# Where the weight slots and the feed-forward tiles begin in SBUF, modulo 512 bytes

## The reference, cut to what matters

```python
for i in range(DEPTH):            # first block
    h = rms_norm(x, attn_norm_g[i])
    q, k, v, u, vv = split(h @ w_in[i])
    merged = concat(rms_norm(gqa_attention(q, k, v)), rms_norm(spatial_gating(u, vv)))
    x = x + merged @ w_o[i]
    h = depthwise_conv(rms_norm(x, ffn_norm_g[i]) @ w_up[i])     # 2 x 2816 columns, 3 taps
    x = x + (silu(gate) * up) @ w_down[i]
for i in range(DEPTH):            # second block
    z = rms_norm(x) @ w_in_2[i]
    mix = concat(dilated_attention, conformer_conv, gated_deltanet)(z)
    x = x + rms_norm(mix @ w_out_2[i])
    h = rms_norm(x)
    x = x + rms_norm((silu(h @ w_gate_2[i]) * (h @ w_up_2[i])) @ w_down_2[i])
```

## Time and profile before

| | |
|---|---|
| median of 3 runs | 2637.12 us (2636.78 to 2638.16) |
| the profiled execution | 2636.79 us |
| its span, first to last instruction | 2635.0 us |
| TensorE busy | 2551.0 us, 97% |
| VectorE, ScalarE, GpSimd busy | 57%, 42%, 5% |
| mean granted TensorE clock | 0.989 of full speed |
| read from HBM | 205.34 MB, 79 GB/s over the span |

### The profile page before, as it was taken

The page is one execution under the profiler, slowest core; times in us unless marked ns, Lnnn a source line. Parts: engine busy times, 40 slices in busy tenths (PEclk is TensorE's granted clock), DMA queues, the critical chain, the costliest instruction groups (busy, mean ns, idle before and its releaser), DMA issues.

```text
span 2635.0 us, 36784 instructions
## 1 busy us (share of the span) xinstructions
PE 2551.0 (97%) x12956; PEld 2021.1 (77%) x12966; DVE 1514.5 (57%) x1957; ACT 1105.3 (42%) x1602; POOL 134.1 (5%) x119
## 2 busy tenths in 40 slices
PE   7999999999999999999998899999899999899998
PEld 5767888887668888887678778888676787688886
DVE  4656755756556746656975554344559755543444
ACT  4554433435554424432475443232424754431323
POOL 1000000000000000000212010000102120100000
PEclk9999999999999999999999999999999999999998
DMA  4203332333113333342220223333221201233333
GB/s 133 72 1 89 98 108 87 99 93 93 49 33 92 102 93 96 100 115 64 56 65 11 64 77 104 91 96 106 55 77 52 65 18 56 72 101 90 96 99 92
DMA packets 394592, 208.04 MB, mean 79 GB/s; under 512 B 9738, under 2 KB 392660, under 8 KB 394484
## 3 DMA queue, kind: packets, MB, share of 16 engines
q1 hardware_dynamic: 391396, 202.79, 26.7%
q0 software_dynamic: 2176, 3.06, 0.5%
q10 hardware_dynamic: 912, 0.77, 0.1%
HBM read 205.34 MB, written 2.10 MB: 79 GB/s over the span
## 4 chain that ended last, share of the span: by engine, by line
PE 89%; DVE 6%; ACT 3%; issue 1%; DMA 0%; SPq 0%; DVEq 0%; ACTq 0%
PE ps L622 65%; PE ps L641 6%; PE ps L899 2%; DVE ps L2773 1%; DVE x_sb L2776 1%; ACT whi L1449 1%; PE ps L1052 1%; PE ps L1067 1%; DVE yc L2497 1%; DVE h_lo L2767 1%; PE ps L1227 1%; PE ps L954 1%; PE ps L1205 1%; PE ps L956 1%; PE ps L955 1%
## 5 line engine op out<-in xcount | busy, mean ns | idle before, releaser
L1449 ACT ACTIVATE whi<-raw 128x1024 fp32r<-128x1024 f32 (+1 forms) x354 | 395.8, 1119 | 1071.2 <-PE ps L622 947.5
L622 PE MATMUL ps<-h_hi,whi 128*128 128x512 f32 x1984 | 789.2, 398 | 4.7 <-ACT whi L1449 4.1
L622 PE MATMUL ps<-h_lo,whi 128*128 128x512 f32 x1984 | 773.7, 390 | 0.0
L622 PE MATMUL ps<-h_hi,wlo 128*128 128x512 f32 x1984 | 530.3, 389 | 0.0
L2095 DVE TENSOR_TENSOR wlo<-raw,whi 128x1024 fp32r<-128x1024 f32 (+1 forms) x354 | 458.7, 1296 | 56.2 <-ACT whi L1449 55.1
L622 PEld LDWEIGHTS ps<-h_hi,whi 128*128 128x128 f32 x1984 | 373.3, 188 | 89.7 <-ACT whi L1449 8.2
L622 PEld LDWEIGHTS ps<-h_lo,whi 128*128 128x128 f32 x1984 | 373.2, 188 | 82.7 <-issue 6.2
L622 PEld LDWEIGHTS ps<-h_hi,wlo 128*128 128x128 f32 x1984 | 372.5, 188 | 77.2
L622 PE MATMUL ps<-a_hi,whi 128*128 128x512 f32 x592 | 230.3, 389 | 0.0
L622 PE MATMUL ps<-a_lo,whi 128*128 128x512 f32 x592 | 230.3, 389 | 0.0
L2808 DVE TENSOR_TENSOR cv<-ps,rstd 128x512 f32<-128x512 f32 x88 | 60.9, 692 | 248.9 <-PE ps L622 241.0
(11 more groups left out here) (408 smaller groups left out, 3281.0 us busy)
## 6 DMA issues: line engine op xcount, KB each, us to landing
raw<-in_w_up SPq DMA_DIRECT2D x132, 512.0 KB, 3.8
raw<-in_w_down SPq DMA_DIRECT2D x64, 704.0 KB, 4.5
raw<-in_w_in SPq DMA_DIRECT2D x82, 512.0 KB, 3.8
raw<-in_w_gate SPq DMA_DIRECT2D x44, 512.0 KB, 3.8
raw<-in_w_o SPq DMA_DIRECT2D x16, 512.0 KB, 3.7
raw<-in_w_out SPq DMA_DIRECT2D x16, 512.0 KB, 3.7
xs<-in_x SPq DMA_DIRECT2D x2, 1024.0 KB, 6.8
out<-xs SPq DMA_DIRECT2D x3, 512.0 KB, 2.9
```

The costliest lines, as they stand in the source:

```text
L622: return pe.matmul(ps[:, ACC[s], :], w[s][:, k, :], r[:, k, :], start=start, stop=stop)
L1449: act.activation(whi[s][:, 0:kt, :], raw[s][:, 0:kt, :], ACT.Copy).then_inc(w_hi_ready.sem, 1)
```

## The change

Dummy tensors are put between others; nothing reads or writes them. The order of `whi` and `wlo` changes from whi0, whi1, wlo0, wlo1 to whi0, wlo0, whi1, wlo1. No instruction is added, removed or moved.

```diff
-        whi = [sb(f"whi{s}", [P, HALF, P], F32R) for s in range(2)]
-        wlo = [sb(f"wlo{s}", [P, HALF, P], F32R) for s in range(2)]
+        whi, wlo = [], []
+        for s in range(2):
+            sb(f"phase{s}", [P, 112])
+            whi.append(sb(f"whi{s}", [P, HALF, P], F32R))
+            wlo.append(sb(f"wlo{s}", [P, HALF, P], F32R))
+        sb("phase_rest", [P, 32])
...
         with ExitStack() as on:
+            sb("phase_a", [P, 32], on=on)
             a_hi = sb("a_hi", [P, HALF, SEQ], F32R, on=on)
             a_lo = sb("a_lo", [P, HALF, SEQ], F32R, on=on)
```

## The result

The changed kernel takes 2668.7 us (median, 2667.62 to 2672.36) against 2637.37 us: 1.0121 times, 95% interval 1.0104 to 1.0139. It is slower by 31 us, 1.2%. The forecast was no change, 2637 us, with its own range of 2632 to 2642; the time lies outside that and inside the whole range of 2610 to 2680, which was wide enough to hold the slower rival.

What follows compares the result with a forecast made beforehand. TensorE, busy 97%, was taken to bound the kernel through 9024 dense matmuls at 226.67 ns. Casts 0 and pitch change 0 x 9024 summed to 0, so 2637 us; own range 2632 to 2642, whole range 2610 to 2680.

Steps and rivals of the forecast that it cites:

- the slower rival: Every `unit`, lines 622 and 641: out-of-phase data stops the stream settling at 226.67 ns; 2674 or 2676 us; chance 0.27.
- The bound: Whole kernel: TensorE busy 97%; 9024 dense matmuls at 226.67 ns pitch are on the path, 9.02 us per ns.
- Weight casts and low parts: ScalarE and VectorE producing `whi` (1060 ns) and `wlo` (1224 ns): out-of-phase source and target cost 0.
- The matmul stream: Dense float32r matmuls: pitch stays 226.67 ns despite new data-to-weight distances; 0 x 9024 = 0, bounds -105 to +120 us.
- I take 0: Dense matmul pitch: no change, since all tiles share one pitch and line 999's short load costs no less.
- the row that I called nearest: The chain's piece of 726 dense matmuls, `h` and `a` tiles, even and odd units: 164.56 us, 226.67 ns each.
- The bounds, 215 and 240 ns: Dense matmul pitch: lowest from the float32 pair, -105 us; highest from the unsettled stretch's longest step, +120 us.
- The rule on ports: TensorE's SBUF reads: moving operand and LDWEIGHTS have independent ports, so by the cited skill page the sum is 0.
- The loss of the settled state: The slower rival: dense stream no longer settles, pitch +4.1 or +4.3 ns, +37 or +39 us; chance 0.27, other slowdowns included.
- The argument against it: Against lost settling: the unsettled stretch after a float32 matmul had the settled one's phases, so phase alone doesn't make the state.
- The faster rival: Dense matmuls: the 13.3 ns are the two reads meeting in phase and go; 2532 us if all reach 215 ns; chance 0.20.

Runs made afterwards that it cites:

- 64-column runs: `unit` loads 64 weight columns instead of 128, half of each output tile left out: 2659.61 us with the addresses of the kernel before, 2662.47 us with the changed kernel's.

## Why the prediction was wrong

**The bound.** Right: the loss is in the pitch of the dense matmuls and lands on the end nearly whole. 3.9 ns of mean pitch x 9024 = 35 us, of 31 measured; the scale of 9.02 us for each nanosecond held within what waiting and unsettled stretches took off.

**Weight casts and low parts.** Right: 1060 and 1224 ns before and after.

**The matmul stream.** Here the forecast failed, in the step "I take 0", on both of its reasons. The first was that h and a tiles, hi and lo, both slots all had one pitch at many addresses. All of them had distance 0, so they were one sample and not six; the row that I called nearest held nothing on the question. What the runs showed in place of 0 is +2.1, +6.5, +6.7 and +0.4 ns at the distances 64, 128, 192 and 256, the mean of the dense pitch going from 227.0 to 230.9 ns. The second was that the short load of line 999 costs no less than the long one, so that the two reads would not meet. The 64-column runs show the inference void: there too the shorter load costs more in phase (230.0 against 226.67), and its pitch still depends on the distance. The bounds, 215 and 240 ns, held; the measured classes lie between 227 and 233. The upper one was a reading of starts rounded to 10 ns: the longest step of that unsettled stretch is 236 ns, the shortest 224.

**The rule on ports.** The rule from the Trainium skill, page "SBUF — State Buffer", section "Who interferes with whom", that TensorE's two read ports are independent and only the VectorE and GpSimd pair contends, does not cover this kernel. Nothing but the distance between the two operands' addresses was changed, by one side or by the other, and the pitch moved by up to 7.4 ns; moved together, it did not. The measurement decides.

**The rivals.** The loss of the settled state was what happened, priced at 230.8 to 231.1 ns, +37 to +39 us; measured were 230.9 ns and +31 us. The whole was mis-sized by what before already paid in unsettled stretches, 3 us, and by the 2.7 us of waiting that went. That the mean pitch met the price is luck: it is the mean of 228.8, 233.1, 233.3 and 227.0, and no class ran at the price. The argument against it, that the unsettled stretch of before had the same phases as the settled one, was true and beside the point: with a good phase the stream settles within nine steps, with another it does not within a unit. I gave this rival 0.27. Line 999, a product at mixed distances that did not settle, was the one row with another distance; it deserved to be the row that I leaned on.
The faster rival failed: of the eight residues none is under 226.67 at 512 columns. The 216 ns that the Trainium skill's page "TensorE: Matmul & The Clock Gate", section "Back-to-back issue gap", gives for a single warm matmul of 512 columns were reached at no phase.

**What stays open.** That the streamed data and the weight load meet in SBUF, every 256 bytes, is the reading that fits: the effect needs both addresses, repeats, changes with the load's length, and is gone at half clock (426 or 427 ns at distances 288 and 352, as at 0). No run shows the meeting itself, and why the cycles have the lengths that they have is not explained. Nor were distances finer than 32 bytes tried.

## What to carry to other kernels

Before calling addresses harmless, ask at how many distances the trace has the two operands: rows that agree because all share one alignment are one sample. Where float32r matmuls run back to back on 512 columns with 128-column loads, keep data and weights in phase modulo 256 bytes, and look at the pitch again whenever a tensor is put ahead of them, or tile sizes change: the good phase of one shape isn't that of another. A change of distance from one matmul to the next costs as well (steps of 232 to 241 ns at the crossings, where only `whi` was out of phase).

## What the runs showed of the hardware

- The pitch of a float32r matmul (512 columns, 128-column load) depends on the distance of its operands modulo 256 bytes: 226.67 ns at 0, 229 at 64, 232 to 234 elsewhere on a 32-byte grid; this kernel, 97% TensorE, lost 53 us to it at the worst (2692.29 against 2639.65, one execution each). The weight block that counts is the one being loaded beside the stream. At the lower granted clock, 0.50, distances 288 and 352 cost nothing.
- The stream has memory: out of a gap or a change of distance it passes through steps of 224 to 241 ns, and either comes to rest or goes round a cycle, of two to seven steps in the full-length runs.
- The excess over the streaming time at distance 0, 13.3 ns, is the same at 256 and at 512 columns.
